# Eight experts in order of load, with 256 to 128 slots instead of 256 each, their weights fetched by an address from a register

## The reference, cut to what matters

```python
def moe_swiglu(h, router, w1, w3, w2):
    probs = jax.nn.softmax((h @ router).astype(jnp.float32), axis=-1)
    top_p, top_i = lax.top_k(probs, TOP_K)                  # TOP_K = 2
    top_p = top_p / jnp.sum(top_p, -1, keepdims=True)
    gates = jnp.sum(jax.nn.one_hot(top_i, N_EXPERTS) * top_p[..., None], axis=-2)
    y = jnp.zeros(h.shape, jnp.float32)
    for e in range(N_EXPERTS):
        y = y + gates[..., e:e + 1] * swiglu(h, w1[e], w3[e], w2[e])
    return y

def swiglu(h, w1, w3, w2):
    return (jax.nn.silu(h @ w1) * (h @ w3)) @ w2
```

## Time and profile before

| What | Value |
|---|---|
| Median of the runs | 2710.22 us |
| The profiled execution's own time | 2724.16 us |
| Its span | 2722.3 us |
| PE busy | 2521.7 us, 93% |
| PE weight loads busy | 2197.1 us, 81% |
| DVE busy | 1401.3 us, 51% |
| ACT busy | 1128.5 us, 41% |
| Chain that ended last, share of PE | 83% (DVE 8%, ACT 3%, issue 3%, DMA 1%) |
| First matmul of the experts, to the last of expert 7 | 1910.84 to 2685.5 us |

### The profile page before, as it was taken

One profiled execution on the slowest core, in us unless ns is written; L12 is line 12 of the kernel. 1 busy time (PEld: TensorE's weight loads), 2 busy tenths in 40 slices (PEclk: granted clock), 3 DMA queues, 4 the chain that ended last, 5 costly groups with the idle time before them and its releaser, 6 DMA issues.

```text
span 2722.3 us, 68039 instructions
## 1 busy us (share of the span) xinstructions
PE 2521.7 (93%) x30324; PEld 2197.1 (81%) x30324; DVE 1401.3 (51%) x2474; ACT 1128.5 (41%) x2126; POOL 146.1 (5%) x163
## 2 busy tenths in 40 slices
PE   6998799898899999989987999998999999999996
PEld 3996577676798999969965777766899999999995
DVE  2337455556533333362374665474565555555565
ACT  3226544544421211242255545444444444444452
POOL 0002000010000000010010010001000000000011
PEclk8999899999999999999998999998999999999998
DMA  7223023320122222222200222202765666566672
GB/s 273 78 78 127 24 74 96 96 75 27 70 77 72 78 78 78 72 72 78 78 11 1 66 66 66 65 5 109 240 209 178 214 212 207 183 211 211 181 259 83
DMA packets 82701, 304.58 MB, mean 112 GB/s; under 512 B 9376, under 2 KB 9504, under 8 KB 82272
## 3 DMA queue, kind: packets, MB, share of 16 engines
q1 hardware_dynamic: 71072, 257.93, 29.6%
q0 software_dynamic: 11328, 42.21, 4.2%
HBM read 273.11 MB, written 27.00 MB: 110 GB/s over the span
## 4 chain that ended last, share of the span: by engine, by line
PE 83%; DVE 8%; issue 3%; ACT 3%; DMA 1%; POOL 0%; SPq 0%; another core or an unknown queue 0%; DVEq 0%; ACTq 0%; POOLq 0%
PE ps L451 19%; PE ps L452 19%; PE ps L453 19%; PE ps L1183 7%; PE ps L812 3%; PE ps L917 2%; PE ps L464 2%; PE ps L1115 2%; PE ps L960 1%; PE ps L976 1%; DMA ring<-in_blocks 1%; PE ps L463 1%; DVE arena L2474 1%; DVE arena L2473 1%; PE ps L1167 1%
## 5 line engine op out<-in xcount | busy, mean ns | idle before, releaser
L2278 DVE TENSOR_TENSOR ring_lo<-ring,w_ffn 128x1024 fp32r<-128x1024 f32 x264 | 322.5, 1225 | 214.5 <-ACT w_ffn L1702 208.5
L451 PE MATMUL ps<-hg_hi,w_ffn 128*128 128x256 f32 x1408 | 402.5, 286 | 3.2 <-DVE hg_lo L2909 3.2
L452 PE MATMUL ps<-hg_lo,w_ffn 128*128 128x256 f32 x1408 | 398.0, 283 | 0.0
L453 PE MATMUL ps<-hg_hi,ring_lo 128*128 128x256 f32 x1408 | 397.5, 282 | 0.0
L1702 ACT ACTIVATE w_ffn<-ring 128x1024 fp32r<-128x1024 f32 x264 | 278.1, 1057 | 197.7 <-PE ps L453 196.2
L451 PEld LDWEIGHTS ps<-hg_hi,w_ffn 128*128 128x128 f32 x1408 | 267.4, 190 | 4.8 <-DVE hg_lo L2909 3.4
L452 PEld LDWEIGHTS ps<-hg_lo,w_ffn 128*128 128x128 f32 x1408 | 266.5, 189 | 1.2
L453 PEld LDWEIGHTS ps<-hg_hi,ring_lo 128*128 128x128 f32 x1408 | 267.0, 190 | 0.0
L1183 PEld LDWEIGHTS ps<-arena 64*64 64x64 f32 x7680 | 165.0, 135 | 98.1 <-issue 78.5
L453 PE MATMUL ps<-hT_ffn_hi,ring_lo 128*128 128x320 f32 x704 | 216.0, 307 | 0.0
L1183 PE MATMUL ps<-arena 64*64 64x64 f32 x7680 | 190.5, 222 | 22.6 <-issue 22.2
(11 more groups left out here) (375 smaller groups left out, 5107.1 us busy)
## 6 DMA issues: line engine op xcount, KB each, us to landing
ring<-in_blocks SPq DMA_DIRECT2D x484, 512.0 KB, 3.7
h_rows<-arena POOLq DMA_DIRECT2D x16, 512.0 KB, 10.2
arena<-h_rows POOLq DMA_DIRECT2D x7, 1024.0 KB, 9.9
...
out_y_all<-x POOLq DMA_DIRECT2D x5, 512.0 KB, 3.7
...
```

Source lines behind the costliest of these rows:

```text
L451: nc.tensor.matmul(dst, w_hi, m_hi, start=start, stop=False)
L452: nc.tensor.matmul(dst, w_hi, m_lo, start=False, stop=False)
L453: return nc.tensor.matmul(dst, w_lo, m_hi, start=False, stop=stop)
L2278: V.tensor_tensor(ring_lo[:, n % RING, :], ring[:, n % RING, :], high[:, n % high.shape[1], :], ALU.subtract).then_inc(*E.sig("w_lo"))
```

## The change

The experts take places 0 to 7 by load, the fullest first, ties by number. Place p has 256, 240, 208, 192, 176, 160, 144, 128 slots; the second path is entered if an expert has more tokens than its place has slots. DVE works out the order in `route_phase` (25 instructions in place of 10 between the count and the remaining `htok_lo`), and writes the 8 expert numbers to `flag_i`. SP waits for them before the first block of the experts, loads them into registers, and adds the register to the address of each block.

`up` has two matmuls for a chunk in place of three: the hi part of the weights against hi and lo of the tokens side by side (2n columns for n slots, in two halves of a bank), and the lo part of the weights against hi (n columns). The two halves are added afterwards by a `tensor_reduce` on DVE, one for w1 and one for w3. The results rotate through banks 4, 5, 6; the transposes for the next expert have bank 7 alone. `down` has as many tiles of slots as the place needs: two for places 0 to 6 (the second with fewer rows), one for place 7, and so has `combine`. The flag of the second path is loaded after the first expert in place of before it. The plain copy to `h_plain` is started behind the first expert's results and the fetch for place 2.

```diff
+RANK_CAP = [256, 240, 208, 192, 176, 160, 144, 128]
...
             for n in range(N_BLOCKS):
+                if n == MOE_FIRST:
+                    sp.wait_ge(sem["rt_rank"], 2)
+                    expert = [sp.value_load(flag_i[0:1, 1 + p:2 + p], min_val=0, max_val=NE - 1) for p in range(NE)]
...
+                    p, c = divmod(n - MOE_FIRST, EXP_B)
+                    sp.dma_start(ring[:, n % RING, :], blocks[bass.ds(expert[p] * EXP_B + (MOE_FIRST + c), 1)].rearrange("n p d -> p (n d)")).then_inc(ring_sem[n % RING], 16)
...
             def up(k, f):
-                hi, lo = hg(k)
-                if f >= 2:
-                    pe.wait_ge(sem["eh_lo"], hidden_before(k) + f - 1)
+                m, n = hg(k), slots(k)
                 for w in range(2):
+                    if 2 * f + w >= 3:
+                        pe.wait_ge(sem["up_ev"], up_before(k, f, w) - 2)
                     w_h, w_l = split_blk(w_ffn)
+                    both = halves(up_bank(f, w), n)
                     for kc in range(KC):
                         c = slice(kc * P, (kc + 1) * P)
-                        mm = mm_split(nc, ps[:, 4 + f % 2, w * CAP:(w + 1) * CAP], w_h[:, c], w_l[:, c], hi[:, kc, :],
-                                      lo[:, kc, :], kc == 0, kc == KC - 1)
+                        nc.tensor.matmul(both, w_h[:, c], m[:, :, kc, 0:n], start=kc == 0, stop=False)
+                        mm = nc.tensor.matmul(both[:, 0, :], w_l[:, c], m[:, 0, kc, 0:n], start=False, stop=kc == KC - 1)
...
             def down(k, g):
-                for s in range(2):
-                    slots = slice(s * P, (s + 1) * P)
+                for s, rows in tiles(k):
+                    r = slice(s * P, s * P + rows)
...
+            def hidden(k, f, more):                      # on VectorE
+                first, n = FFN_AT[1] + k * EXP_B, slots(k)
+                t, u, v = ftmp[:, f % 2, 0:n], u_sum[:, 0:n], v_sum[:, 0:n]
+                dve.wait_ge(sem["block_used"], first + up_at(f, 0) + 1)
+                V.tensor_reduce(u, summed(up_bank(f, 0), n), AX.X, ALU.add).then_inc(*E.sig("up_ev"))
+                w_lo(w_ffn, first + up_at(f, 0) + 3)
+                dve.wait_ge(sem["block_used"], first + up_at(f, 1) + 1)
+                dve.wait_ge(sem["eh_lo"], hidden_before(k) + f)
+                V.tensor_reduce(v, summed(up_bank(f, 1), n), AX.X, ALU.add).then_inc(*E.sig("up_ev"))
                 dve.wait_ge(sem["eh_th"], hidden_before(k) + f + 1)
-                V.scalar_tensor_tensor(t, t, 1.0, b[:, 0:CAP], ALU.add, ALU.mult).then_inc(*E.sig("dve_step"))
+                V.scalar_tensor_tensor(t, t, 1.0, u, ALU.add, ALU.mult).then_inc(*E.sig("dve_step"))
...
-                pool.dma_start(h_plain.rearrange("(i p) d -> p i d", p=P), htok[:, :, :]).then_inc(sem["h_out"], 16)
...
+                    if e == 0:
+                        pool.dma_start(h_plain.rearrange("(i p) d -> p i d", p=P), htok[:, :, :]).then_inc(sem["h_out"], 16)
```

More of the change, by code:

```diff
@@ L40 @@
 CAP = 256
+RANK_CAP = [256, 240, 208, 192, 176, 160, 144, 128]
+RANK_AT = [0, 1, 2, 3, 4, 5, 6, 7]
+CAPS = [RANK_CAP[r] for r in RANK_AT]
+Y_AT = [sum(CAPS[:p]) for p in range(NE)]
 ROWS = 640
@@ L366, in build @@
         yrow = take(NT * NE, i=NT, e=NE)
+        above = take(NE * NE, e=NE, q=NE)
+        place = take(NE * NE, e=NE, q=NE)
+        ptmp = take(2 * NE * NE, b=2, e=NE, q=NE)
+        key, rank, pos, cap_e, eid, over_e, y_base = (take(NE) for _ in range(7))
+        last_rk, last_gate = take(NT), take(NT)
         pick = take(2 * NT, w=2, i=NT)
@@ L414, in hg, with slots, tiles, tiles_before @@
         def hg(k):
-            return (hg_hi1, hg_lo1) if k < NE and k % 2 else (hg_hi0, hg_lo0)
+            return hg1 if k < NE and k % 2 else hg0
+        def slots(k):
+            return CAPS[k] if k < NE else CAP
+        def tiles(k):
+            return [(s, min(P, slots(k) - P * s)) for s in range((slots(k) + P - 1) // P)]
+        def tiles_before(e):
+            return sum(len(tiles(k)) for k in range(e))
+        LAST_TILES = len(tiles(NE - 1))
+        def out_before(n):
+            return 2 * (LAST_TILES + 2 * (n - 1)) if n else 0
+        def turns_before(n):
+            return out_before(n) // 2
+        def up_bank(f, w):
+            return 4 + (2 * f + w) % 3
+        def up_at(f, w):
+            return 2 * f + w + max(0, f - 1)
+        def up_before(k, f, w):
+            return 2 * FE * k + 2 * f + w
+        def halves(bank, n):
+            return ps[:, bank, 0:2 * n].rearrange("p (h n) -> p h n", h=2)
+        def summed(bank, n):
+            return ps[:, bank, 0:2 * n].rearrange("p (h n) -> p n h", h=2)
+        u_sum, v_sum = ftmp[:, 0, CAP:2 * CAP], ftmp[:, 1, CAP:2 * CAP]
         def early(e, f):
@@ L2920, in hidden @@
-                for n in ahead(f)[0]:
-                    w_lo(w_ffn, first + n)
+                V.scalar_tensor_tensor(v, t, 0.5, v, ALU.mult, ALU.mult).then_inc(*E.sig("eh_g"))
+                if more or f < FE - 1:
+                    w_lo(w_ffn, first + up_at(f, 1) + 3)
                 dve.wait_ge(sem["eh_hi"], hidden_before(k) + f + 1)
                 dve.wait_ge(sem["eh_g"], hidden_before(k) + f + 1)
-                V.tensor_tensor(ge_lo[:, f % 2, :], g, ge_hi[:, f % 2, :], ALU.subtract).then_inc(*E.sig("eh_lo"))
@@ L2925, in hidden @@
-                for n in ahead(f)[1]:
-                    w_lo(w_ffn, first + n)
+                V.tensor_tensor(ge_lo[:, f % 2, 0:n], v, ge_hi[:, f % 2, 0:n], ALU.subtract).then_inc(*E.sig("eh_lo"))
+                if f >= 1 and (more or f < FE - 1):
+                    w_lo(w_ffn, first + up_at(f, 1) + 4)
             def out_lo(n):
-                for m in range(4):
-                    dve.wait_ge(sem["ey_ev"], 4 * n + m + 1)
+                for m in range(4 if n else 2 * LAST_TILES):
+                    dve.wait_ge(sem["ey_ev"], out_before(n) + m + 1)
@@ L2972, in moe_expert @@
                 if e < NE - 1:
-                    for n in range(3):
-                        w_lo(w_ffn, first + EXP_B + n)
+                    w_lo(w_ffn, first + EXP_B + 2)
                 else:
@@ L2984, in moe_pass @@
                 for f in range(FE):
-                    hidden(k, f)
+                    hidden(k, f, k not in LAST_PASS)
                     if f == FE // 2 and k not in LAST_PASS:
-                        select(k + 1, n + 1, (k + 1) % NE, CAP * ((k + 1) // NE))
-                if k not in LAST_PASS:
-                    w_lo(w_ffn, first + EXP_B)
-                    w_lo(w_ffn, first + EXP_B + 1)
+                        select(k + 1, n + 1, (k + 1) % NE, CAP * ((k + 1) // NE - 1))
                 out_lo(n)
```

234 lines of the change are left out of this document (127 added, 107 removed).

## The result

The changed kernel takes 2603.44 us (median of 4 runs, 2598.30 to 2610.21), beside 2714.34 us of the kernel before in the same session (4 runs, 2710.10 to 2721.21). The ratio is 0.959, with a 95% interval of 0.956 to 0.962. The profiled execution took 2610.21 us, its span is 2608.3.

| Part of the span | Before, us | After, us | Difference |
|---|---|---|---|
| Up to the first matmul of the experts | 1910.84 | 1916.46 | +5.6 |
| Places 0 to 6 | 678.54 | 587.70 | -90.8 |
| Place 7, to the first `combine` matmul | 99.53 | 71.67 | -27.9 |
| From there to the end | 33.4 | 32.5 | -0.9 |

A forecast was written before the change was run, and what follows sets the result against it. The prediction took the experts to be bound by PE; 95.4 + 15.3 + 1 + 9 - 11 - 5 - 0.5 + 2 = 106 us off the 2710.2 us median gave 2604 us, range 2565 to 2655.

The forecast's parts named there:

- Up: Chunks of `up` on PE: 2311.8 ns against 2853.6 summed over the places, 176 times, 95.4 us less.
- floor: Least time for a pair of weight load and matmul on PE, whatever its columns: 111 to 119 ns, taken as 118.9.
- that sign: Spacing of a chunk's second matmul: 111 to 119 ns at every n for the forecast, falling to 58 at n = 128 otherwise.
- rival A: Matmuls of `up`: no least time, loads hide wherever they are shorter than what runs; 2571 us, chance 12%.
- Down and place 7: Place 7: one tile in `down` saves 15.3 us, its smaller gather 1 us; DVE taking over gives 11 us back.
- An expert's end: Last `down` of each expert: late lo part asked for earlier, about 0.2 us of a 1.3 us wait stays, 9 us less.
- Reductions and transfers: DVE reductions, two per step, 0.69 us each at n = 256, stay hidden in place 1 and 6; faster weight transfers lose nothing.
- Routing: Before expert 0: added DVE instructions and SP's wait for expert numbers delay the gather; 5 us lost, bounds 0 and 14.
- B: Expert steps become a chain of waits, 0.5 us in each of 77 steps, 38 us: 2642 us, chance 14%.
- C: Second matmul of chunks below 256 columns runs slowly: 102 us more (2706) or 250 us more (2854), chance 5% each.
- D: Second path entered because an expert has more tokens than slots: sixteen passes of about 90 us, 4050 us, chance 1%.

The follow-up runs named there:

- The two experiments that change only columns or only loads: Against the changed kernel: narrow matmul cut to 64 columns, 2600.0 us (0.957); wide matmul loading 64 of 128 weight columns, 2582.3 us (0.950).
- three in a row: Changed kernel with its wide matmul of 2n columns split in two of n, so three matmuls per chunk of `up`: 2662.5 us, ratio 0.980.
- the old order: Changed kernel with the last w2 block's lo part again behind the gated product on DVE in each expert's last step: 2616.6 us, ratio 0.963.
- the kernel with the written order: Changed kernel with the order of experts written into the program, SP neither waiting for the router nor loading registers: 2599.6 us, ratio 0.955.

## Why the prediction came out

**Up.** Predicted 95.4 us less. The chunks after sum to 2307 ns over the eight places, predicted 2312. The model of a chunk (columns of the wide matmul plus one floor) holds within 5 ns at every n. What was wrong is where the floor would show: the prediction looked for it in the spacing behind the narrow matmul, and the records put it behind the wide one. Who had read that sign alone would have taken rival A. The two experiments that change only columns or only loads settle it. The range for the floor was 111 to 119: three in a row show 111, and in the pair with a wide matmul the chunk less its wide columns leaves 115 to 122. In place 7 it leaves 127, but 116 without the slow chunks. The Trainium skill (TensorE: Matmul & The Clock Gate, section Back-to-back issue gap) has 81 ns at 128 columns; with these operands the runs show 111, so the trace disagrees with it, as the prediction had taken it to. The 238 ns that the prediction works out from these 81 ns, an estimate, come to 223 when done again (81 ns or the columns for each narrow matmul, whichever is more), 39 us and not 42; no term of the sum hangs on it.

**Down and place 7.** Place 7 went from 99.5 to 71.7 us, 27.9 less. The prediction's parts for it were 118.9 ns x 176 = 20.9, 15.3 for the tile, 1.1 for its end, 1 to 2 for the shorter last lo parts, less the 11 of DVE: 28. The sum agrees better than its parts do: of the 1.1 at its end only 0.45 came (a wait of 0.92 us in place of 1.37), and a step with a taking back takes 6.9 to 7.0 us where nothing else disturbs it, not 7.2. The 1.17 us that the prediction has for a `w_lo` don't stand in the earlier trace rows, which have 1.226. That place 7 is held by DVE was right in the profile after, but only half of the cause: taking 0.75 us off each step on DVE gave nothing, since the order on ACT and the gathers' buffers come right behind.

**An expert's end.** 9 predicted, 8 of it in places 0 to 6. The last two `down` start 3.28 to 2.94 us apart, where it was 4.30: 1.0 to 1.4 less in each of seven. The waits listed for places 1 to 6 are 0.7 us in all, and the old order brings 6.6 back.

**Reductions and transfers.** Hidden, as predicted, at the duration of the line (0.657 against 0.65). Blocks at 248 GB/s in place 6, with no wait of PE for one.

**Routing.** Predicted 5 late, measured 3.2 after the count. The mechanism is right, its parts not: the loads of a register take 0.27 us each after the first, not 0.47, though with what stands between them the eight last 4.6 us from 1891.6; ACT's first eviction came 15.5 us after the count (predicted 14.6); PE stalled for 3.98. In return the stalls of before (3.16 and 2.24) shrank to 0.93, for which the expected 0-to-14 range had allowed. A part that the prediction missed is the clock: behind the stall PE ran for 5.7 us at a granted clock of 0.50, that is 1.2 GHz, with 213 ns for a matmul of the gather and not 120. That makes the stall's price 6.3 us, as the kernel with the written order shows, and not 4. The kernel before had a slow stretch too, 3.7 us at the start of expert 0, which made that expert 98.54 us long where the others took 96.67. These 1.9 us have gone with the change, which makes its routing cost some 1.3 us net where the sum has 5.

**The copy.** The prediction gave its move no gain of its own except through those stalls. No trace shows it to be worth anything.

**The rivals.** B didn't occur: PE's waits in places 1 to 6 are 0.7 us. Nor did C: narrow matmuls below 256 columns run at 0.45 ns a column or hide under a load. D: no second path is entered.

The sum was 106 us, 2604; the medians of one session differ by 111, the spans by 114. That 2604 meets the measured 2603.4 so closely is luck: the sum is 5 us short, and the median that it starts from, 2710.2, lies 4 below the 2714.3 of all four runs. The 8 us more in the spans lie in places 0 to 6: 90.8, where the terms give 74.4 for `up`, 7.9 for the ends and 1 for the smaller gather of place 7. The largest part of the difference is a term that was too small, the chunk before. Its 356.7 ns are three times 118.9, and these come from 47 spacings that leave out the first of the step. The first chunk of a block took 391 ns and the others 354 to 362, so the mean of experts 1 to 6 is 361.0: 5.3 us in seven places. Expert 0's slow clock has 1.9, chunks shorter than forecast after the change have 1.0; the ends and transposes gave 0.7 more, `down` 1.4 less. The start of the experts (5 predicted, 5.6 measured) agrees only because 2.4 us of it lie ahead of the count. The load of the flag, 0.5 in the sum, costs 0.1 at most: in the kernel with 256 slots in seven places, place 0, which has the load behind it, takes 94.17 us and the next two take 94.07 and 94.10.
